# Half of the next expert's first low part moves behind the second low part of the turned hidden rows, in a hybrid retention, SSD and mixture-of-experts layer on one core

## What is computed

```python
def expert_block(args):
    tok, e = args
    xb = h_pad[tok]
    hid = jax.nn.silu(xb @ w_gate[e]) * (xb @ w_up[e])
    return hid @ w_down[e]

yb = lax.map(expert_block, (slot_tok.reshape(n_blocks, MOE_BLOCK), blk_expert))
out = jnp.zeros((T + 1, d), h.dtype).at[slot_tok].add(yb.reshape(cap, d) * slot_w[:, None])
```

## Time and profile before

| | us |
|---|---|
| median of 3 runs | 2374.65 (2372.53 to 2376.19) |
| the profiled execution, its time | 2371.26 |
| the profiled execution, its span | 2369.6 |
| PE busy in the span | 2183.6 (92%) |
| DVE busy | 1414.7 (60%) |
| ACT busy | 1054.4 (44%) |
| all low parts of expert weights, L2518, x192 | 431.0 |
| all high parts of expert weights, L2470, x192 | 356.5 |

### The profile page before, as it was taken

The page is one execution under the profiler, slowest core; times in us unless marked ns, Lnnn a source line. Parts: engine busy times, 40 slices in busy tenths (PEclk is TensorE's granted clock), DMA queues, the critical chain, the costliest instruction groups (busy, mean ns, idle before and its releaser), DMA issues. The chain is left out here.

```text
span 2369.6 us, 35396 instructions
## 1 busy us (share of the span) xinstructions
PE 2183.6 (92%) x11582; PEld 1830.7 (77%) x11583; DVE 1414.7 (60%) x2099; ACT 1054.4 (44%) x1518; POOL 648.3 (27%) x647
## 2 busy tenths in 40 slices
PE   8999999999998779997999849999999999999890
PEld 5888888899997668886888737778788888887770
DVE  6322222376565678886577754765766665647776
ACT  4422321242223036665233224755666665547763
POOL 0000000000000668886122222322333333323323
PEclk9999999999999999998999959999999999999995
DMA  8623333555552986665553244997988987768997
GB/s 305 240 99 117 125 152 133 167 171 191 174 173 74 374 325 229 219 219 180 178 205 139 102 137 134 345 289 237 340 259 256 278 267 244 242 170 265 350 351 302
DMA packets 297516, 518.78 MB, mean 219 GB/s; under 512 B 33406, under 2 KB 206022, under 8 KB 292664
## 3 DMA queue, kind: packets, MB, share of 16 engines
q1 hardware_dynamic: 271000, 439.52, 54.4%
q0 software_dynamic: 17216, 44.60, 8.4%
q10 hardware_dynamic: 9216, 33.56, 3.5%
HBM read 397.28 MB, written 129.09 MB: 222 GB/s over the span
## 5 line engine op out<-in xcount | busy, mean ns | idle before, releaser
L2518 DVE TENSOR_TENSOR e_w_low<-e_w_whole,e_w_high 128x2048 fp32r<-128x2048 f32 x192 | 431.0, 2286 | 92.5 <-ACT e_w_high L2470 90.7
L2470 ACT ACTIVATE e_w_high<-e_w_whole 128x2048 fp32r<-128x2048 f32 x192 | 356.5, 1909 | 43.4 <-DMA e_w_whole<-in_moe_w_down_dram 18.7
L2411 PE MATMUL e_pG<-e_w_high,e_xT 128*128 128x512 f32 x768 | 306.0, 398 | 1.2 <-ACT e_xT L2463 1.2
L2412 PE MATMUL e_pG<-e_w_low,e_xT 128*128 128x512 f32 x768 | 305.7, 398 | 0.0
L856 PE MATMUL proj_acc<-w_high,hT_high 128*128 128x512 f32 x672 | 263.8, 393 | 0.0
L856 PE MATMUL proj_acc<-w_low,hT_high 128*128 128x512 f32 x672 | 262.2, 390 | 0.0
L856 PE MATMUL proj_acc<-w_high,hT_low 128*128 128x512 f32 x672 | 262.0, 390 | 0.0
L2420 PE MATMUL e_pY<-e_w_high,e_hT 128*128 128x512 f32 x768 | 227.0, 407 | 13.0 <-ACT e_hT L2482 13.0
L2415 PE MATMUL e_pG<-e_w_high,e_xT 128*128 128x512 f32 x768 | 195.3, 396 | 0.0
L1189 DVE SCALAR_TENSOR_TENSOR conv_out<-ch,cw,conv_out 128x258 f32<-128x258 f32 x288 | 120.4, 482 | 96.9 <-ACT conv_out L767 96.7
L2411 PEld LDWEIGHTS e_pG<-e_w_high,e_xT 128*128 128x128 f32 x768 | 145.5, 189 | 37.0 <-issue 1.6
(11 more groups left out here) (300 smaller groups left out, 4175.5 us busy)
## 6 DMA issues: line engine op xcount, KB each, us to landing
e_w_whole<-in_moe_w_gate_dram SPq DMA_DIRECT2D x64, 1024.0 KB
e_w_whole<-in_moe_w_up_dram SPq DMA_DIRECT2D x64, 1024.0 KB
e_w_whole<-in_moe_w_down_dram SPq DMA_DIRECT2D x64, 1024.0 KB
by_token<-tok SPq DMA_DIRECT2D x32, 512.0 KB, 3.0
w_in_raw<-in_w_mod_dram SPq DMA_DIRECT2D x32, 512.0 KB, 4.0
m_tok<-by_token SPq DMA_DIRECT2D x16, 768.0 KB, 5.5
s_kv<-by_token SPq DMA_DIRECT2D x20, 512.0 KB, 5.8
modulated_high<-hT_high SPq DMA_DIRECT2D x9, 1024.0 KB, 3.9
```

Of the source, the lines that this page charges most:

```text
L2411: nc.tensor.matmul(pG[:, half], xT[:, 0, k], wh[:, half, w], start=(k == 0), stop=False)
L2412: nc.tensor.matmul(pG[:, half], xT[:, 0, k], wl[:, half, w], start=False, stop=False)
L2470: nc.scalar.activation(wh[:, third, part], raw[:, third, part], ACT.Copy).then_inc(whs.sem, 1)
L2518: nc.vector.tensor_tensor(wl[:, third, part], raw[:, third, part], wh[:, third, part].bitcast(F32), ALU.subtract).then_inc(wls.sem, 1)
```

## The change

DVE's `low(following, 0)` is split. Its first instruction stays between the hidden rows of half 0 and half 1. The second moves behind the low part of the second pair of turned rows, just ahead of `low(following, 1)`. No instruction is added or removed, and SP's, ACT's, PE's and POOL's programs are the same; their waits name the same counts.

```diff
+            def low_half(e, third, n):
+                part = slice(n * HALF, (n + 1) * HALF)
+                dve.wait_ge(whs.sem, whs.at(e, 2 * third + n + 1))
+                nc.vector.tensor_tensor(wl[:, third, part], raw[:, third, part], wh[:, third, part].bitcast(F32), ALU.subtract).then_inc(wls.sem, 1)
+
             def low(e, third):
-
-                for n in range(2):
-                    part = slice(n * HALF, (n + 1) * HALF)
-                    dve.wait_ge(whs.sem, whs.at(e, 2 * third + n + 1))
-                    nc.vector.tensor_tensor(wl[:, third, part], raw[:, third, part], wh[:, third, part].bitcast(F32), ALU.subtract).then_inc(wls.sem, 1)
+                low_half(e, third, 0)
+                low_half(e, third, 1)
...
                     if following is not None and half == 0:
-                        low(following, 0)
+                        low_half(following, 0, 0)
...
                 if following is not None:
+                    low_half(following, 0, 1)
                     low(following, 1)
```

## The result

| | before | the change |
|---|---|---|
| median, us | 2374.08 (2371.85 to 2376.19, 5 runs) | 2384.02 (2381.79 to 2387.01, 5 runs) |
| ratio | | 1.0041, 95% interval 1.0030 to 1.0052 |
| span of the profiled execution | 2369.6 | 2382.7 |

A second set, against 13 runs of before, gave 1.0034 (1.0023 to 1.0046). The forecast was 2390.4 in a range of 2378 to 2400, so the sign is as forecast, and the size is 9.9 us instead of 15.7.

What follows compares the result with a forecast made beforehand. PE was taken as the busiest engine, with loads pacing the streaks. Pairs 8.2 plus streaks 7.5 made 15.7 us on 2371.3, so 2387.0 profiled and 2390.4 us as a median, range 2378 to 2400.

Steps and rivals of the forecast that it cites:

- What moves, and when: In each of 31 last blocks, SP issues the load of third 0 5.2 us later; the other moves cost nothing.
- The cover of third 1: Third 1's low part starts 0.86 us later at no cost, covered by 1.6 us of PE's products with third 0.
- Pairs: Four places with two last blocks in a row: third 0's late load costs 2.0 us each, 8.2 in all.
- the 10.3 us for a load: Assumed length of third 0's load in pairs, chosen between bounds of 8.8 and 11.6 us.
- The first rival: Delayed loads still land in time and the 5.2 us hidden-row wait goes: 2369.5 us as a median; chance 0.05.
- My own formula: In pairs, issue at 1732.2 plus load length plus 4.3 us gives PE's down products: 1746.8 instead of 1744.76.
- The 8.8 us bound: Least length of third 0's load, from its issue until the DMA engines fell idle at about 1735.8.
- my signs of being wrong: SP's issue moves without ACT waiting in pairs, the streaks' period changes, or PE waits for low parts ahead of L2411.
- the rival: PE waits for third 0's low part at each next expert's first product, margin 0.24 us: +9.3 on top, 2399.7; chance 0.13.
- Streaks: Three runs of successive last blocks, paced by loads: 3.0 us late less 0.5 regained, 2.5 each, 7.5 in all.
- The hole at the start of the stream: About 2.2 us of idle DMA engines before third 1's load; it closes, cutting a streak's lateness from 5.2 to 3.0.
- The bound's logic: PE's waits, 13.0 us for turned rows and 5.2 for hidden rows, cap any gain; loads pace the streaks.

Runs made afterwards that it cites:

- the second trace: The unaltered change executed and profiled once more against before: 2382.94 us against 2373.88, +9.1.
- the cut loads: Each third's load issued in two halves, ACT awaiting whole thirds: 2366.14 us on before, 2367.2 on the change; ACT awaiting halves: 2360.43 and 2365.38.
- the half bytes: Each load of a third brings only half its rows: 2344.24 us on before, 2345.42 on the change.
- the two later loads: Load of third 0 issued only after third 1's first low part: 2400.0 us in the order of before, 2408.14 in that of the change.
- the earlier release alone: Before with each third's load issued in two halves as each low part is made, ACT still awaiting the whole third: 2366.14 us.
- the later load: The change, with SP issuing third 0's load only after third 1's first low part: 2408.14 us against 2374.33, +33.8.
- the delay alone: Before, VectorE's order kept, with SP issuing third 0's load only after third 1's first low part: 2400.0 us against 2373.4, +26.6.

## Why the prediction was right, and where its sizes were off

- **What moves, and when: right.** The load starts 3.63 us behind the second transposes, forecast 3.66 (1732.2 - 1728.54). The cover of third 1 held in a sound block, and the wait for hidden rows shrank from 5.2 to 1.8 us, forecast gone. PE's wait for ACT's turned rows, forecast at some 34 us, is 14.9.
- **Pairs: the term that was mis-sized**, 8.2 us forecast, 1.3 measured (2.2 in the second trace). The step that failed is "the delayed load starts while the block's gather runs, as the old one overlapped it, so I change nothing for that", and with it the 10.3 us for a load. It took 8.3, below the 8.8 that I had called its least, and 8.2 to 8.4 in the other three pairs. The first rival, whose condition was a load under 8.0 us, was missed by 0.3 us and not by 2.3. My own formula with 8.3 gives 1732.2 + 8.3 + 4.3 = 1744.8 against 1744.76, 0.04 us; measured 0.03. What made it shorter I read from POOL's rows, first of before, then of the change:

```profile
1727.70 1.04 POOL L2330 DMA_INDIRECT e_x<-second_norm,e_ids  x1 [4.81 <-DMA rows_summed<-e_y,e_rows_held]
1736.44 2.08 POOL L2319 COPY e_rows_held<-e_rows_held 128x6 int32<-128x6 int32 x1 [7.69 <-DMA e_x<-second_norm,e_ids]
```

```profile
1737.79 1.04 POOL L2330 DMA_INDIRECT e_x<-second_norm,e_ids  x1 [4.80 <-DMA rows_summed<-e_y,e_rows_held]
1742.84 1.50 POOL L2319 COPY e_rows_held<-e_rows_held 128x6 int32<-128x6 int32 x1 [4.00 <-DMA e_x<-second_norm,e_ids]
```

In before the gather of the next rows was issued 0.67 us after the load, and took 8.7 us beside it. In the change it runs alone, takes 5.1, and has ended when the load's bytes begin to flow. The other pairs agree: the two loads that took 12.2 and 12.0 us beside 0.98 MB of the software queue took 8.3 and 8.2 without any. No run moves the gather alone, so this cause is read from the traces and not tested. In the DMA view of the load's 9.2 us (1742.3 to 1751.5) the software queue doesn't appear, where the earlier trace rows had 0.52 MB of it:

```profile
GB/s 0 0 0 0 93 89 183 232 312 356 383 387 383 378 365 325 370 370 374 356 378 347 370 356 356 356 347 338 347 352 347 347 307 294 285 289 276 347 329 352
...
q1 hardware_dynamic: 2655, 2.69, 92.6%
```

- The 8.8 us bound was wrong for the same reason. It was the length of that load beside a gather, and I used it as the least for one without.
- **What the pairs did lose** I had costed at nothing: third 1, whose load now stands behind third 0's. ACT waits 2.35 us for it, and PE loses up to 0.5 us a block later. The cover I gave was for making the low part, not for the load behind it. One of my signs of being wrong came by this, a wait of PE for low parts ahead of L2411: 0.33 us, but for third 1, and not for third 0 as in the rival.
- **Streaks: 7.5 us forecast, 7.0 measured** (10.5 in the second trace). The hole at the start of the stream closed, as forecast: from 2163.5 to 2180 us of the change no slice of 0.75 us moves less than 199 GB/s, where before had its three low slices. The sum fits, the parts less well (2.7, 3.3 and 1.0), and I had left out a cost, the clock, so that part of the fit is luck. That the loads' lateness is the cause is shown by the cut loads and the half bytes. How much of the 7.0 is the clock's isn't shown, but the traces bound it. Over the last streak, blocks 42 to 48, the lateness is 9.7, 11.5, 10.3, 11.5, 9.9, 11.3 and 9.8 us. Each rise holds a fall of the clock, and the block behind it gives 1.2 to 1.6 us back, since the loads set the pace. Only a fall in the last stalled block of a streak is kept. That happened in the first two streaks, whose last blocks lost 1.2 and 1.9 us, so an estimate from these is at most 3 us of the 7.0.
- **The bound's logic held**: no run gives a sign that the hidden rows' earlier start is worth anything on its own. With half the bytes the orders are equal.
- **The page's rule.** By the Trainium skill, "SBUF — State Buffer", "The DMA setup-cost knee", the load of third 0 would take an estimated 6.8 us. The rows here give 8.2 to 8.4 us in the change, and 8.5 to 8.7 with the two later loads, from issue to ACT's start for loads without a gather beside them: above the rule, yet nearer to it than my 10.3 was.

## What to carry to other kernels

Where one buffer is refilled as soon as a slow pass over it ends, moving the pass moves the transfer, and that is the first thing to price, before the engine's own order. Slack hides such a move up to a point, and behind it the rest is paid at each use: here a load 5.1 us later cost 9.9 us in all, one 6.6 us later 26.6. A load's length read beside other traffic is no bound for the moved one: ask which of the other transfers it will meet at its new place. And if a buffer is used up in halves, release and await it in halves: that took 13.5 us off here, of which 7.7 came with the earlier release alone, without touching any engine's arithmetic.

## What the runs showed of the chip that I had not expected

The granted clock of TensorE. In before it stood at the higher of its two levels (2.4 GHz) over all of 1440 to 2310 us, with PE idle for at most 1.67 us at a time. In the change it fell to 1.2 GHz for 3.4 us in six places of the streaks, each within 1.4 us of the end of an idle stretch of 2.05 to 2.13 us. One of them, PE's timeline:

```profile
1506.84 0.73 PE L2420 MATMUL e_pY<-e_w_high,e_hT 128*128 128x512 f32 x2 [2.06 <-ACT e_hT L2482]
1507.40 1.02 PE L2420 MATMUL e_pY<-e_w_low,e_hT 128*128 128x512 f32 x2
1508.22 1.05 PE L2420 MATMUL e_pY<-e_w_high,e_hT 128*128 128x512 f32 x2
```

Two products take 1.05 us instead of 0.63. An idle stretch as long doesn't always bring it: the second trace of the change has seven of 2.0 to 2.15 us, and the clock fell at five. With the later load one of 3.03 us, at 2240 us, passed at the higher level. The price shows best with the later load, in whose four pairs PE was idle for 2.15 to 2.33 us each. These are ten microseconds around each of them (after the busy times of the engines: granted clock, DMA share, GB/s):

```profile
1760.00:1770.00 10.00, 7.77 (x34) 6.12 (x33) 5.96 (x6) 6.79 (x7) 2.19 (x1) 0.83 1.07 330
1818.00:1828.00 10.00, 7.85 (x40) 6.29 (x40) 6.87 (x6) 6.67 (x7) 2.12 (x1) 1.00 1.06 324
1876.00:1886.00 10.00, 7.76 (x33) 6.17 (x32) 6.39 (x6) 6.94 (x8) 2.22 (x1) 0.83 1.06 338
1972.00:1982.00 10.00, 7.67 (x29) 5.96 (x27) 7.77 (x7) 7.22 (x8) 2.30 (x1) 0.83 1.05 347
```

Three pairs met the lower level and lost 4.0, 4.0 and 4.1 us; the one that kept the higher lost 2.5. So by these four places a fall cost 1.5 to 1.7 us on top of the wait. The accident in the first block is the same thing: PE was idle there for 2.95 us before its transposes (2.65 in before, at the higher level), the clock fell, and 1.6 us were lost. I don't count them as an effect of the change, for its second trace has 1.90 us of idle time there, no fall and no loss, while the delay alone, in the order of before, has 2.54 us, the fall and the same 1.6 us lost.

```profile
1428.10 0.44 PE L2399 MATMUL e_pH<-ident,e_hid 128*128 128x128 f32 x2 [2.95 <-DVE e_hid L2529]
```
